# Memory's keys made with tokens in the partitions: a change in one stage of a two-block transformer kernel

## The reference, cut to what matters

```python
def memory_cross_attention_branch(q, gate, mem_h, w_mem_kv, qn_g, kn_g, w_proj):
    k, v = jnp.split(mem_h @ w_mem_kv, 2, axis=-1)          # mem_h: 256 tokens x 1024
    q = rms_norm(q.reshape(B, S, X_HEADS, X_HEAD_DIM), qn_g)
    k = rms_norm(k.reshape(B, M, X_HEADS, X_HEAD_DIM), kn_g) # 4 heads of 256
    ...
def rms_norm(x, g, eps=1e-6):
    y = x * lax.rsqrt(jnp.mean(x * x, axis=-1, keepdims=True) + eps)
    return y * g
```

## Time and profile before

| | us |
|---|---|
| median of 3 executions | 1691.04 |
| the three executions | 1688.78, 1691.04, 2245.79 |
| the profiled execution, its own time | 1690.89 |
| its span | 1689.2 |
| TensorE busy in the span | 1603.5 (95%) |
| VectorE, ScalarE, GpSimd busy | 996.7, 725.1, 190.2 |

### The profile page before, as it was taken

How to read it: one execution, slowest core, us unless ns; L and a number is a source line. 1 busy time by engine, 2 the same in 40 slices (tenths; PEclk the granted TensorE clock), 3 DMA queues, 4 the chain that set the end, 5 groups by cost and what they waited for, 6 DMA issues and landing times. The chain is left out here.

```text
span 1689.2 us, 24321 instructions
## 1 busy us (share of the span) xinstructions
PE 1603.5 (95%) x9944; PEld 1263.7 (75%) x9944; DVE 996.7 (59%) x1676; ACT 725.1 (43%) x1155; POOL 190.2 (11%) x158
## 2 busy tenths in 40 slices
PE   6999989999999999899999899989998999999997
PEld 5776876788878776677778787767766787888886
DVE  4999975456655477647444747776546453334445
ACT  6533347335522467647632525545423332232212
POOL 2433445400010000000004100000000000000000
PEclk9999999999999999999999999999999999999999
DMA  5222234444455322222234232210002332323231
GB/s 204 88 88 87 78 110 125 162 162 149 133 171 174 118 82 88 77 99 74 82 119 144 63 119 75 75 39 4 3 26 76 107 118 87 95 93 97 91 100 50
DMA packets 45645, 166.07 MB, mean 98 GB/s; under 512 B 5264, under 2 KB 5392, under 8 KB 45536
## 3 DMA queue, kind: packets, MB, share of 16 engines
q1 hardware_dynamic: 42912, 155.95, 28.8%
q0 software_dynamic: 2624, 8.59, 1.7%
HBM read 162.42 MB, written 2.10 MB: 97 GB/s over the span
## 5 line engine op out<-in xcount | busy, mean ns | idle before, releaser
L569 PE MATMUL bank<-h_T_hi,weight_hi 128*128 128x512 f32 x1208 | 496.2, 411 | 5.0 <-DVE h_T_lo L2085 2.8
L604 ACT ACTIVATE weight_hi<-raw 128x1024 fp32r<-128x1024 f32 x241 | 254.9, 1057 | 559.4 <-PE bank L571 553.4
L612 DVE TENSOR_TENSOR weight_lo<-raw,weight_hi 128x1024 fp32r<-128x1024 f32 x184 | 225.5, 1225 | 443.4 <-ACT weight_hi L604 443.4
L570 PE MATMUL bank<-h_T_lo,weight_hi 128*128 128x512 f32 x1208 | 480.2, 398 | 0.0
L571 PE MATMUL bank<-h_T_hi,weight_lo 128*128 128x512 f32 x1208 | 480.1, 397 | 0.0
L569 PEld LDWEIGHTS bank<-h_T_hi,weight_hi 128*128 128x128 f32 x1208 | 229.1, 190 | 66.8 <-issue 11.7
L570 PEld LDWEIGHTS bank<-h_T_lo,weight_hi 128*128 128x128 f32 x1208 | 229.3, 190 | 56.3 <-issue 5.6
L571 PEld LDWEIGHTS bank<-h_T_hi,weight_lo 128*128 128x128 f32 x1208 | 228.6, 189 | 55.6
L2080 DVE SCALAR_TENSOR_TENSOR bank<-conv_in,columns,bank 128x512 f32<-128x512 f32 x240 | 181.4, 756 | 8.3
L612 POOL TENSOR_TENSOR weight_lo<-raw,weight_hi 128x1024 fp32r<-128x1024 f32 x57 | 138.6, 2437 | 200.5 <-ACT weight_hi L604 200.4
L569 PE MATMUL bank<-branch_hi,weight_hi 128*128 128x512 f32 x192 | 76.0, 396 | 1.4 <-DVE scratch_more L2080 1.4
(11 more groups left out here) (448 smaller groups left out, 2320.8 us busy)
## 6 DMA issues: line engine op xcount, KB each, us to landing
raw<-in_weights SPq DMA_DIRECT2D x289, 512.0 KB, 3.5
x_in<-in_x SPq DMA_DIRECT2D x4, 512.0 KB, 5.7
x_rows<-in_x POOLq DMA_DIRECT2D x4, 512.0 KB, 4.9
out<-x_rows SPq DMA_DIRECT2D x4, 512.0 KB, 2.6
mem_in<-in_mem POOLq DMA_DIRECT2D x2, 512.0 KB, 8.4
ln_rows<-in_ln_g POOLq DMA_DIRECT2D x4, 256.0 KB, 3.8
ln_rows<-in_ln_b POOLq DMA_DIRECT2D x4, 256.0 KB, 4.5
silu_row<-in_c POOLq DMA_DIRECT2D x1, 512.0 KB, 11.4
```

What stands on the lines that cost most here:

```text
L569: pe.matmul(o, lhs[0], rhs[0], start=start, stop=False)
L570: pe.matmul(o, lhs[0], rhs[1], start=False, stop=False)
L604: act.activation(parts[n % SPLIT][0][:, :], raw[u % RAW][:, :], ACT.Copy).then_inc(*weight_hi.up(u))
L612: engine.tensor_tensor(lo[:, :], raw[u % RAW][:, :], view(hi[:, :]), ALU.subtract).then_inc(*ready.up(u))
```

## The change: what it does

The keys' eight tiles become token units, in two halves of 512 features (two heads), four pairs each. The first half stands before `conv_gate 7`, the second after `merge 7`. With tokens in the partitions the sum of squares of a head is along the free axis, and ScalarE makes it with the accumulator of its `Square` (`squares`), four instructions for a half. The root is taken of a 128x4 tile. VectorE scales rows (`dve_key_rows`) into a scratch tile, TensorE turns them back (`pe_key_turn`, eight transposes for a half), and ScalarE and VectorE make the high and low parts from the turned bank with the gain as a scale. The first half's rows are scaled after tap 20 of the last channel tile. ScalarE's order of weights, values and roots in `act_keys` is new, and one `exp_table` moves to `act_cross`, behind the first gate.

```diff
@@ unit_plan
-        for i in (0, 1) if last else ():
-            f(("xk", i), "w_mem_kv", i * P)
+        if last:
+            t(("xk", 0), "w_mem_kv", 0)
         f(("conv_gate", n), "w_in", W_IN_AT["conv_gate"] + n * P)
-        for i in (2, 3) if last else ():
-            f(("xk", i), "w_mem_kv", i * P)
         f(("merge", 0, n), "w_in", W_IN_AT["merge"] + GATE_OF[0] * D + n * P)
-    for n in range(4, KT):
-        f(("xk", n), "w_mem_kv", n * P)
+    t(("xk", 1), "w_mem_kv", 512)
@@ banks
-    mem_places, key_places, key_sums = bank_ring((6, 7)), bank_ring((6, 7, 1)), bank_ring((2,))
+    mem_places, key_places = bank_ring((6, 7)), bank_ring((6, 7, 6, 7, 2, 1, 6, 7))
@@ TensorE
+    def pe_key_pair(pe, half, pair, out_banks):
+        token_unit(pe, ("xk", half), pair, out_banks, mem_T, lambda t: key_places.take(pe, ("xk", half, t), key_rows, half, t))
+
+    def pe_key_turn(pe, half):
+        for t in range(MT):
+            pe.wait_ge(*key_rows.at(half, t))
+        for h in (2 * half, 2 * half + 1):
+            key_places.take(pe, ("xk turned", h), norm_lo, "xk", h, 1)
+            for c in range(2):
+                for t in range(MT):
+                    done = pe.transpose(key_turned_bank(h, c)[:, cut(t)], norm_ring["xk", half, t][:, cut(2 * (h % 2) + c)], ident[:, :])
+            done.then_inc(*key_turned.up(h))
...
-        pe_key_units(pe, 0)
-        feature_unit(pe, ("conv_gate", n), unit_bank(pe, ("conv_gate", n)), h_T, mid=at_gate)
-        pe_key_units(pe, 1)
+        out_banks = []
+        for pair in range(KT // 2):
+            pe_key_pair(pe, 0, pair, out_banks)
+        feature_unit(pe, ("conv_gate", n), unit_bank(pe, ("conv_gate", n)), h_T)
...
     def pe_keys(pe):
-        pe_key_units(pe, 2)
-        pe_key_units(pe, 3, mid=lambda: pe_conv_mean(pe, KT - 1))
-        pe_key_sum(pe, 2)
+        out_banks = []
+        for pair in range(KT // 2):
+            pe_key_pair(pe, 1, pair, out_banks)
+            if pair == 0:
+                pe_key_turn(pe, 0)
+            if pair == 2:
+                pe_conv_mean(pe, KT - 1)
...
-                for n in range(3 * pair, min(3 * pair + 3, KT)) if half == 0 else ():
+                if half == 0 and pair == 1:
+                    pe_key_turn(pe, 1)
+                for n in range(3 * pair - 3, min(3 * pair, KT)) if half == 0 and pair else ():
                     pe_conv_squares(pe, n)
@@ ScalarE, act_keys after the change, in full from conv_b 7 on
+        act_conv_out(act, n - 1)
+        feed_hi(act)
+        feed_hi(act)
+        feed_hi(act)
+        squares(0)
+        root(0)
+        act_take(act, ("conv_gate", n), conv_gates[:, n, :], ACT.Silu)
+        feed_hi(act)
+        act_take(act, ("merge", 0, n), y_T[:, n, :], ACT.Sigmoid)
+        feed_hi(act)
+        feed_hi(act)
+        key_hi(0)
+        act_conv_out(act, n)
+        feed_hi(act)
+        feed_hi(act)
+        for n in range(2):
+            centred_squares(n)
+        feed_hi(act)
+        squares(1)
+        root(1)
+        feed_hi(act)
...
         act.wait_ge(*norm_lo.at("xk", X_HEADS - 1, 1))
         for n in range(KT):
             silu(n)
-            if n < 5:
+            if n < 3:
                 feed_hi(act)
-        exp_table(act)
-        values(1)
+            if n == 5:
+                values(1)
@@ VectorE
-            if n == KT - 1 and j == 14:
-                dve_key_full(dve, 0)
-            if n == KT - 1 and j == 18:
-                dve_key_lo(dve, 0)
+            if n == KT - 1 and j == 20:
+                dve_key_rows(dve, 0)
...
+    def dve_key_rows(dve, half):
+        dve.wait_ge(*key_rooted.at(half))
+        for t in range(MT):
+            for m in range(2):
+                r = spot("xk", half, "r", n=4)[:, 2 * t + m:2 * t + m + 1]
+                done = dve.tensor_scalar(norm_ring["xk", half, t][:, cut(m, X_DIM)], key_places["xk", half, t][:, cut(m, X_DIM)], r, None,
+                                         ALU.mult)
+            done.then_inc(*key_rows.up(half, t))
@@ dve_keys
-        dve_key_full(dve, 1)
-        dve_key_lo(dve, 1)
-        for n in range(KT):
-            centre(n)
-        dve_key_full(dve, 2)
-        dve_key_lo(dve, 2)
-        dve_key_full(dve, 3)
-        dve_key_lo(dve, 3)
+        dve_key_lo(dve, 0)
+        for n in range(5):
+            centre(n)
+        dve_key_rows(dve, 1)
+        for n in range(5, KT):
+            centre(n)
+        dve_key_lo(dve, 1)
```

More of the change, by code:

```diff
@@ L148, in unit_plan @@
     return plan
-TAKEN_BY = {"conv_b": "act", "conv_a": "dve", "conv_gate": "act", "merge": "act", "proj": "dve", "xk": "dve",
+TAKEN_BY = {"conv_b": "act", "conv_a": "dve", "conv_gate": "act", "merge": "act", "proj": "dve",
             "xq": "dve", "x_gate": "act", "dq": "dve", "dk": "dve", "d_gate": "act", "pu": "act",
             "ffn_g": "act", "ffn_u": "dve"}
-TILES = {"xv": MT, "dv": TT, "w_out": TT, "pv": TT, "w_out_2": TT, "ffn_out": TT}
+TILES = {"xk": MT, "xv": MT, "dv": TT, "w_out": TT, "pv": TT, "w_out_2": TT, "ffn_out": TT}
 class Signal:
@@ L301, in build @@
     eps = usable("eps", [P, 4])
-    small = usable("small", [P, 352])
+    small = usable("small", [P, 376])
     mod = usable("mod", [P, 6, KT])
@@ L1549, in act_keys, with squares, root, key_hi @@
     def act_keys(act):
[L1550 to L1562, removed]
+        def squares(half):
+            for t in range(MT):
+                o = norm_ring.take(act, ("xk", half, t), key_turned, 2 * half + 1)
+                act.wait_ge(*product.at("xk", half, "tile", t))
+                for m in range(2):
+                    activate(act, o[:, cut(m, X_DIM)], key_places["xk", half, t][:, cut(m, X_DIM)], ACT.Square,
+                             accum=spot("xk", half, "sq", n=4)[:, 2 * t + m:2 * t + m + 1]).then_inc(*act_own.up())
+        def root(half):
+            act.wait_ge(*act_own.last())
+            act_root(act, spot("xk", half, "r", n=4), spot("xk", half, "sq", n=4), spot("xk", half, "ln", n=4), 1.0 / X_DIM, EPS6,
+                     key_rooted.up(half))
+        def key_hi(half):
+            for h in (2 * half, 2 * half + 1):
+                act.wait_ge(*key_turned.at(h))
+                for c in range(2):
+                    activate(act, k_x[0][:, 2 * h + c, :], key_turned_bank(h, c), ACT.Copy, scale=column("x_kn_g", c)).then_inc(
+                        *norm_hi.up("xk", h, c))
         def centred_squares(n):
@@ L1598, in act_keys @@
         feed_hi(act)
+        feed_hi(act)
[7 more added lines that the diff above has]
+        squares(1)
         root(1)
+        feed_hi(act)
+        centred_squares(2)
+        centred_squares(3)
         key_hi(1)
         feed_hi(act)
[L1602 to L1611, removed]
         centred_squares(4)
-        feed_hi(act)
         centred_squares(5)
-        root(3)
-        key_hi(3)
         feed_hi(act)
         centred_squares(6)
-        feed_hi(act)
         centred_squares(7)
-        feed_hi(act)
         r = conv_r_ring.take(act, 0, conv_normed, KT - 1)
@@ L1687, in act_cross @@
                 feed_hi(act)
+                exp_table(act)
             feed_hi(act)
@@ L2164, in dve_taps, with dve_key_lo @@
                     dve_turned(dve, "mem", mem_T, "mem_norm_g", 0, k)
[L2166 to L2175 removed]
+    def dve_key_rows(dve, half):
+        dve.wait_ge(*key_rooted.at(half))
+        for t in range(MT):
+            for m in range(2):
+                r = spot("xk", half, "r", n=4)[:, 2 * t + m:2 * t + m + 1]
+                done = dve.tensor_scalar(norm_ring["xk", half, t][:, cut(m, X_DIM)], key_places["xk", half, t][:, cut(m, X_DIM)], r, None,
+                                         ALU.mult)
+            done.then_inc(*key_rows.up(half, t))
+    def dve_key_lo(dve, half):
+        for h in (2 * half, 2 * half + 1):
+            dve.wait_ge(*norm_hi.at("xk", h, 1))
+            for c in range(2):
+                fused(dve, k_x[1][:, 2 * h + c, :], key_turned_bank(h, c), column("x_kn_g", c), view(k_x[0][:, 2 * h + c, :]), ALU.mult,
+                      ALU.subtract).then_inc(*norm_lo.up("xk", h, c))
     def dve_keys(dve):
```

35 lines of the change are left out of this document (4 added, 31 removed).

## The result

| | before | after |
|---|---|---|
| median, us | 1690.64 (4 runs) | 1668.11 (4 runs, 1666.0 to 1669.52) |
| ratio | | 0.9869, 95% interval 0.9853 to 0.9885 |
| span of the profiled execution | 1689.2 | 1667.1 |
| first key unit begins | 205.56 | 205.14 |
| `proj 0` begins | 311.09 | 301.65 |

One of the four executions of the kernel before took 2245.79 us; the ratio leaves it out and compares 1668.11 with 1690.24.

What follows compares the result with a forecast made beforehand. TensorE, busy 95% of the span, was taken as the bound. Out 16.0 us (waits, hand-offs, slow clock, key sums), in transposes 1.8 and waits 5.75: net 8.5, 8.9 by the walk; 1690.89 - 8.7 gave 1682, range 1677 to 1690.

Steps and rivals of the forecast that it cites:

- The walk: Step-by-step timing of the new order from 205.56 to `proj 0`, forecast at about 302.2 against 311.09: 8.9 us earlier.
- Step (1): First half's key pairs end at 216.76; TensorE idles 2.6 us for GpSimd's weights, starting the gate at 219.35.
- steps (2): First half's root is done at about 223.2, 9 us early; VectorE scales rows after tap 20, to 233.2 and 233.9.
- (3): Gate and merge to 231.5, a 1.75 us wait for banks 6 and 7, second-half keys to 246.3; old 2.55 us wait gone.
- Step (4): Second half's squares, root and scaling: turn 1 waits 1.4 us (ends 0 and 2.8), done at 254.2.
- Step (5): Layer norm sums and values' units after turn 1: memory's units end at 277.9 against 285.38, 7.5 us earlier.
- Step (6): ScalarE's silu loop: weights of `x_gate 1` made at about 291, ready at 294.5, just covering TensorE's need at 294.7.
- Step (7): Query's root with its table load made ahead: `proj 0` starts at about 302.2, its 1.4 us wait nearly gone.
- (a): Rival: clock falls after shorter stretches or in a later stage, 1.7 us each, and turn 1 late: 1687; chance 0.17.
- (b): Rival: after 311, modulation transfers or VectorE set the pace, so the 8.9 us is waited off: 1689 to 1691; chance 0.13.
- (d): Rival: TensorE stays at 1.2 GHz from the gate through the following pairs, up to 1697.5 us; chance 0.05.
- (c): Rival: fewer new waits, shorter squares, turn 1 on time, no clock loss: 1678 to 1680; chance 0.15.

Runs made afterwards that it cites:

- Experiments 8: The changed kernel with one `feed_hi` of `act_keys` moved ahead of `act_conv_out(6)`, so the gate's weights are made earlier: 1670.5 us, ratio 0.9876.
- 11: Experiment 5's kernel with one `feed_hi` ahead of `act_conv_out(6)` and the first half's rows scaled after tap 14 instead of 20: 1659.0 us.
- Experiment 2: The changed kernel with `small` at 384 words in place of 376, activations again 96 bytes behind a multiple of 128: 1681.9 us, ratio 0.9942.
- Experiment 1: The kernel before with only `small` widened from 352 to 376 words: 1679.7 us, ratio 0.9931.
- experiments 3: The kernel before with `small` at 360 words, activations at a multiple of 128 bytes: 1666.1 us, ratio 0.9856.
- 5: The changed kernel with `x_gain` and `one_minus_ka` moved into unused words, so activations start at a multiple of 128 bytes: 1654.4 us, ratio 0.9783.
- 6: The kernel before, packed like experiment 5, 64-byte pad ahead of the weight parts, `small` at 376: weights and activations both 64 bytes off; 1665.9 us.
- 12: The kernel before, packed like experiment 5, 32-byte pad ahead of the weight parts, `small` at 376: both operands 32 bytes off; 1667.1 us.
- experiments 1 and 7: Experiment 7: the kernel of experiment 6 with `small` at 360 words, weights 64 bytes off and activations at a multiple of 128: 1686.0 us, ratio 0.9978.
- experiments 2 and 4: Experiment 4: the kernel before with `small` at 368 words, activations 32 bytes behind a multiple of 128: 1690.7 us, ratio 1.0009.
- experiment 10: Experiment 3's kernel with only `exp_table` moved behind the first gate of `act_cross`: 1665.2 us, ratio 0.9852.

## Why the prediction was right in its place and wrong in its sum

**The stage.** The walk stood 0.5 us off after 96: `proj 0` at 302.2 forecast, 301.65 measured. Step (1): a wait of 2.6 us before the gate behind GpSimd; it is 2.67, and the gate begins at 219.17 for 219.35. The clock fell behind it, as forecast (0.68 over 220 to 224), and steps (2) and (3) hid that: the second half begins at 233.28, forecast 233.25, with 0.4 us of waiting left. No wait near 246. The mean's last sum at 242.63, forecast 243.5 less its own 0.9. Experiments 8 and 11 show that the reason was right too: take the waits away and the taps hold the stage at nearly the same places. How close the single waits came has luck in it. Experiment 2 has the same order, and its profiled execution waited 0.83 us before the gate and 1.78 before the second half, with no slow clock between:

```profile
217.94 0.47 PE L567 MATMUL bank<-h_T_hi,weight_hi 128*128 128x512 f32 x1 [0.83 <-POOL weight_lo L610]
...
232.03 0.47 PE L567 MATMUL bank<-weight_hi,mem_T_hi 128*128 128x512 f32 x1 [1.78 <-DVE scratch_more L2174]
```

The second half was held by VectorE's row scaling there too, 1.2 us earlier than in the changed kernel, so the mechanism stands and the split between the two waits does not. Besides, six of the stage's units move `h_T`, and their shorter pitch is some 0.6 us of the changed kernel's 301.65, which the walk did not have.

Step (4) was half a term off: turn 1 waited 0.7, not 1.4, since a square with its accumulator reading came every 0.35 us, not 0.6. (The walk had this wait at 0 if a square took 0.33; at 0.35 it was still 0.7.) Behind the last square, the table load of the root took 1.28 us (from 249.09) and the next activation began 0.01 us after it, so charging 1.28 was right here. Three rows of ScalarE from half 1, the reading overlapped by the next square:

```profile
247.51 0.36 ACT L579 ACTIVATE scratch<-bank 128x256 f32<-128x256 f32 x1
247.78 0.19 ACT L579 ACTIVATION_READ_ACCUMULATOR scratch<-bank 128x1 f32 x1
247.87 0.37 ACT L579 ACTIVATE scratch<-bank 128x256 f32<-128x256 f32 x1
```

Step (5): memory's units end at 277.55, forecast 277.9. Step (6): the weights of `x_gate 1` are made at 290.21, forecast 291. Step (7): the wait before `proj 0` is 0.21. Transposes: eight of them moved the next unit by 0.8 us (236.15 to 236.94), so the price of 0.11 each from rows 8 held, and not the about 275 ns one after another that the prediction weighed, from the Trainium skill ("TensorE: Matmul & The Clock Gate", section "Part 4: PE-mode transpose").

**The step that failed** is the sentence of the first part: "so I take a shift at 311.09 to reach the end unchanged". It looked only at waits. That the matmuls themselves could take another time behind the stage was not considered, because the edit that did it, `small` from 352 to 376 words, was not in the list of parts at all: it was costed at nothing without being named. The prediction took 1378 us from `proj 0` to the end; the changed kernel took 1365.5, at a pitch of 0.229 in place of 0.233. Experiment 1 prices the edit at 11 us by itself, experiment 2 gives 1681.9 us for the change without it, where the prediction said 1682. The rivals failed with it: (a), (b) and (d) went the other way, and (c), faster than forecast, sought the rest in waits and clock, which gave 0.7 us at turn 1.

**What the rows before could have told.** `v_x` and `p_T` are two activation tiles, both 96 bytes behind a multiple of 128. Two rows of TensorE's timeline of the kernel before, from one of their units:

```profile
409.18 0.39 PE L571 MATMUL bank<-p_T_hi,v_x_lo 128*128 128x512 f32 x1
...
409.86 0.40 PE L571 MATMUL bank<-p_T_hi,v_x_lo 128*128 128x512 f32 x1
```

Three pitches in 0.68 us are 0.227, at the same shape, clock and weight load that gave 0.233 wherever `h_T` meets a weight. I had passed over that difference. It is no perfect sign. The same kind of unit at 467.22, the last head's, had 0.230 to 0.233 between most of its rows. And in experiment 2, where `v_x` and `p_T` again both stand 96 bytes behind a multiple of 128, all units of this kind ran at 0.232 (1.16/5 here):

```profile
398.58 0.40 PE L567 MATMUL bank<-p_T_hi,v_x_hi 128*128 128x512 f32 x1
...
399.74 0.39 PE L569 MATMUL bank<-p_T_hi,v_x_lo 128*128 128x512 f32 x1
```

Why is not known. Against the weights, the activations stand 32 bytes back in the kernel before and 96 bytes on in experiment 2, which is the same modulo 128; so this, too, speaks against the remainder modulo 128 as the whole account.

## What to carry to other kernels

Before pricing a diff's instructions, look for what it does to addresses: a tile that grows by some words in the middle of a layout moves everything behind it, and here 96 bytes were worth 11 to 14 us, more than the whole re-made stage. Compare the pitch of the same dense matmuls in both traces, far from the change; if it differs at the same granted clock, suspect placement, and one run with a pad in the old kernel tests it. Try the moving and the stationary tiles of long matmul streams at the same remainder modulo 512 bytes, as the fastest runs here had them; whether the same remainder modulo 128 is enough was not tried.

## What the runs showed of the hardware

The pitch of 128x512 matmuls with a weight load each depended on how the SBUF start addresses of the two operands stand to each other. Read at the two places of the table it was 0.2267 us with both operands at the same place modulo 512 bytes (experiments 3, 5, 6 and 12), 0.229 with the moving operand 64 bytes further on than the stationary one, 0.233 with these two exchanged (experiments 1 and 7), and 0.233 to 0.234 at 32 or 96 apart (before, experiments 2 and 4), 3% between the ends. It is no complete rule: experiment 7 had 0.234 at 556.68 where the table's place had 0.229, and experiment 2 had 0.232 with two operands at the same remainder. That the reads of the moving operand and of the next stationary one get into each other's way would explain it; no run shows the mechanism. The Trainium skill ("TensorE: Matmul & The Clock Gate", section "Part 2: What happens when you issue a matmul") says that loading the next tile's weights takes no SBUF read bandwidth from the running matmul; the pitches above speak against reading this as independence from placement. The Trainium skill's page "SBUF — State Buffer" (section "Operand start alignment") is about which starts are legal, and all starts used here are.

The waits that experiments 8 and 11 gathered in one place lasted 3.18 and 3.87 us, and behind both the granted clock was at the 1.2 GHz level for a few us (0.50 over 234 to 238 in experiment 8, 0.57 over 241 to 245 in experiment 11). In the changed kernel the wait of 0.41 us at the first place showed no fall, nor did the one of 0.66 at turn 1, and the second place had no wait. The wait of 2.67 us ahead of its gate brought a fall as well (0.68 over 220 to 224), but the slack of the taps hid it; the falls behind 3.18 and 3.87 us stood where nothing did. A wait of such a length does not always bring a fall: behind 2.5 us at the same place the clock was 0.57 in experiment 3 and 1.00 in experiment 10.
